# A mixer stage rearranged: gate products inside the Fourier stage, half a weight tile in each attention round, the mixing shares spread by DMA

## The reference

```python
p = u @ w_in[l]                       # u: normed tokens
y_a = fourier_mix(a_in) @ w_br_a[l]   # 8 groups, 2-D DFT, real part
y_b = dilated_mixture(qb, kb, vb, rel_bias[:, :6]) @ w_br_b[l]   # 3 groups, mixed by softmax over their lse
y_c = diff_attention(qc, kc, vc, ...) @ w_br_c[l]                # 4 heads, dense, p0 - lam * p1
gates = sigmoid(u @ w_gate[l] + b_gate[l])                       # 3 gates of width 1024
merged = gates[0] * y_a + gates[1] * y_b + gates[2] * y_c
x = x + merged @ w_out[l]
```

## Time and profile before

| | |
|---|---|
| Runs | 3716.03, 3720.18, 3720.73 us; median 3720.18 us |
| Profiled execution | 3716.92 us, of which the span from first to last instruction is 3715.1 us |
| PE busy | 3500.0 us (94%), mean granted clock 0.969 |
| DVE, ACT, POOL busy | 1602.1 us (43%), 1379.7 us (37%), 1483.0 us (40%) |
| DMA | mean 83 GB/s over the span |
| Chain that ended last | PE 88%, DVE 7%, ACT 2%, issue 2% |

### The profile page before, as it was taken

How to read it: one execution, slowest core, us unless ns; L and a number is a source line. 1 busy time by engine, 2 the same in 40 slices (tenths; PEclk the granted TensorE clock), 3 DMA queues, 4 the chain that set the end, 5 groups by cost and what they waited for, 6 DMA issues and landing times.

```text
span 3715.1 us, 50014 instructions
## 1 busy us (share of the span) xinstructions
PE 3500.0 (94%) x16502; PEld 2868.8 (77%) x16502; DVE 1602.1 (43%) x2305; ACT 1379.7 (37%) x2382; POOL 1483.0 (40%) x1124
## 2 busy tenths in 40 slices
PE   8999997999999999999989999999988987889997
PEld 6888885778888888878857788887777886568886
DVE  3223525644322432244366443224776666243224
ACT  4233323644322432242346443324473233233322
POOL 3444531345444544454313544444220025125443
PEclk9999998999999999999989999999998998989998
DMA  3222321122222322233212323223110012112222
GB/s 111 98 96 96 122 74 44 63 96 96 94 98 96 102 97 96 97 121 102 68 38 68 102 91 101 96 96 102 63 68 10 10 46 85 46 53 100 96 96 91
DMA packets 87302, 309.10 MB, mean 83 GB/s; under 512 B 9823, under 2 KB 11873, under 8 KB 87060
## 3 DMA queue, kind: packets, MB, share of 16 engines
q1 hardware_dynamic: 82512, 297.97, 23.8%
q10 hardware_dynamic: 4676, 9.62, 0.9%
HBM read 305.38 MB, written 2.17 MB: 83 GB/s over the span
## 4 chain that ended last, share of the span: by engine, by line
PE 88%; DVE 7%; ACT 2%; issue 2%; DMA 0%; ACTq 0%; POOL 0%; DVEq 0%; POOLq 0%; SPq 0%
PE ps L438 26%; PE ps L440 25%; PE ps L439 25%; PE ps L843 1%; PE ps L588 1%; PE ps L852 1%; PE ps L611 1%; PE ps L846 1%; PE ps L913 1%; PE ps L601 1%; PE ps L526 0%; PE ps L752 0%; PE ps L898 0%; DVE x L1743 0%; PE ps L731 0%
## 5 line engine op out<-in xcount | busy, mean ns | idle before, releaser
L403 POOL TENSOR_TENSOR w_lo<-raw,w_hi 128x512 fp32r<-128x512 f32 x1120 | 1482.8, 1330 | 2203.2 <-ACT w_hi L943 1726.9
L438 PE MATMUL ps<-u_hi,w_hi 128*128 128x512 f32 (+1 forms) x2990 | 1172.6, 392 | 37.9 <-POOL w_lo L403 10.4
L439 PE MATMUL ps<-u_hi,w_lo 128*128 128x512 f32 (+1 forms) x2990 | 1156.7, 387 | 0.0
L440 PE MATMUL ps<-u_lo,w_hi 128*128 128x512 f32 (+1 forms) x2990 | 1156.4, 387 | 0.0
L438 PEld LDWEIGHTS ps<-u_hi,w_hi 128*128 128x128 f32 x2990 | 566.9, 190 | 164.6 <-issue 28.6
L439 PEld LDWEIGHTS ps<-u_hi,w_lo 128*128 128x128 f32 x2990 | 566.9, 190 | 113.9 <-issue 4.1
L440 PEld LDWEIGHTS ps<-u_lo,w_hi 128*128 128x128 f32 x2990 | 566.4, 189 | 114.1
L945 ACT ACTIVATE w_hi<-raw 128x512 fp32r<-128x512 f32 x560 | 352.5, 629 | 767.7 <-PE ps L440 767.0
L438 PE MATMUL ps<-m_hi,w_hi 128*128 128x512 f32 x1344 | 530.2, 394 | 14.8 <-DVE m_lo L1477 11.9
L943 ACT ACTIVATE w_hi<-raw 128x512 fp32r<-128x512 f32 x560 | 350.8, 626 | 519.4 <-PE ps L440 483.6
L439 PE MATMUL ps<-m_hi,w_lo 128*128 128x512 f32 x1344 | 525.7, 391 | 0.0
(11 more groups left out here) (424 smaller groups left out, 2765.8 us busy)
## 6 DMA issues: line engine op xcount, KB each, us to landing
raw<-jobs SPq DMA_DIRECT2D x560, 512.0 KB, 3.3
tab<-vec_dram ACTq DMA_DIRECT2D x8, 448.0 KB, 5.0
x<-x_in SPq DMA_DIRECT2D x4, 512.0 KB, 6.8
out<-x SPq DMA_DIRECT2D x8, 256.0 KB, 2.0
tab<-dft_in ACTq DMA_DIRECT2D x2, 901.0 KB, 4.8
tab<-chunk_in ACTq DMA_DIRECT2D x1, 1024.0 KB, 4.9
tab<-mem_in ACTq DMA_DIRECT2D x4, 256.0 KB, 3.0
tab<-vec_dram ACTq DMA_DIRECT2D x4, 128.0 KB, 7.1
```

What stands on the lines that cost most here:

```text
L403: pool.tensor_tensor(w_lo[:, s, w], raw[:, s, w], w_hi[:, s, w].bitcast(F32), ALU.subtract).then_inc(lo_done[s], 1)
L438: pe.matmul(ps[bank][:, 0:n], w_hi[:, s, w], hi[:, k, 0:n], start=k == ks[0], stop=False)
L439: pe.matmul(ps[bank][:, 0:n], w_lo[:, s, w], hi[:, k, 0:n], start=False, stop=False)
L440: last = pe.matmul(ps[bank][:, 0:n], w_hi[:, s, w], lo[:, k, 0:n], start=False, stop=k == ks[-1])
```

## The change

- PE runs seven of the first gate's eight jobs inside `fourier`, one in each of the groups 0 to 6, and the eighth after the first scores of `dense`. Their results go to `pt[:, 0:8]`, where the sigmoid is also taken, in the Fourier stage.
- p and q share one bank (`ps[4 + g % 2]`); the sine part's zero column is dropped, and DVE copies the two elements that belonged to it.
- A dense round carries half a job of the Fourier branch (`half_job`): the first half in an even, the second in an odd round. ACT makes one half of the next weights in each round (`split`).
- Probabilities go into `T[:, 7]`, a tile of their own. `logits(u+2)` no longer waits for the transposes of u; `probabilities(u+1)` waits for them.
- The row transposes are spread over the groups 0 to 4 of `fourier`.
- The shares are not spread by PE: ACT's queue stores them to DRAM after round 1 and loads them to 2x64 partitions after round 3. DVE mixes one group in each of the rounds 6, 8 and 10.
- The loads of the first three bias tables are started after the second exponentials and no longer before the first.
- In the tail one gate job stands before heads 0 and 1 and one before heads 2 and 3; the transposes alternate between `ps[7]` and `ps[6]`; ACT writes `m_hi` and DVE `m_lo` straight from PSUM.
- The weight slices lie in DRAM in the new order. Their number is the same.

PE, a new function, `fourier` and `dense`:

```diff
+            def half_job(s, half, hi, lo, ready):
+                if half == 0:
+                    pe.wait_ge(evac[s], c.take(f"evac{s}"))
+                pe.wait_ge(lo_done[s], c.next(f"lo{s}"))
+                for k in range(half * KT // 2, (half + 1) * KT // 2):
...
             def fourier():
...
                     if g < 7:
                         along_channels(g + 1)
+                    if g == 0:
+                        pe.wait_ge(ut_copied, c.now("ut_copied"))
+                        dilated_row(0)
+                    if g < 5:
+                        dilated_row(g + 1)
+                    if g < 7:
+                        job(g % 2, u_hi, u_lo)
...
-                mix_groups(lambda: scores(0))
+                scores(0)
                 pe.wait_ge(vt_done, c.now("vt_done"))
                 scores(1)
+                job(1, u_hi, u_lo)
+                pe.wait_ge(y_done, c.now("y_done"))
                 for u in range(16):
-                    if u < 14:
+                    if 0 < u < 14:
                         scores(u + 2)
...
-                    if u % 2 == 0:
-                        job(0, u_hi, u_lo)
-                    else:
-                        job(1, m_hi, m_lo, ready=(m_ready, c.now("m")) if u == 1 else None)
+                    transposes(u)
+                    if u == 0:
+                        scores(2)
+                    half_job(u // 2 % 2, u % 2, m_hi, m_lo, ready=(m_ready, c.now("m")) if u < 2 else None)
+                    values(u)
                 c.up("m", 8)
-                job(0, u_hi, u_lo)
-                job(1, u_hi, u_lo)
                 for h in range(4):
+                    if h % 2 == 0:
+                        job(h // 2, u_hi, u_lo)
```

ACT, in `dense`:

```diff
                 for u in range(16):
                     act.wait_ge(tr_full, c.next("tr_full"))
                     act.activation(T[:, 4 + u % 2], ps[4][:, :], ACT.Copy).then_inc(tr_copied, c.up("tr_copied"))
+                    split(1 - u // 2 % 2, u % 2)
                     if u % 2:
-                        gate(T[:, 7], T[:, 7], 0, ACT.Sigmoid, bgate(0, u // 2))
-                    pump(1 - u % 2)
...
+                    if u == 1:
+                        act.wait_ge(mixw_done, c.next("mixd"))
+                        act.dma_start(share_dram, rows_m.rearrange("p g n -> p (g n)")).then_inc(shares_stored, c.up("stored", 16))
+                    if u == 3:
+                        act.wait_ge(shares_stored, c.now("stored"))
+                        for h in range(2):
+                            act.dma_start(shares[64 * h:64 * h + 64].rearrange("p g n -> p (g n)"),
+                                          bass.AP(share_dram.tensor, h * 3 * S, [[0, 64], [1, 3 * S]])).then_inc(shares_in, c.up("shares", 16))
```

DVE, in `fourier` and `dense`:

```diff
             def fourier():
                 for g in range(8):
                     if g:
+                        scaled((g - 1) % 2, pt[:, g - 1])
                         fourier_out(g - 1)
...
+                    if g == 6:
+                        dilated_shares(0)
+                        dilated_shares(1)
+                    if g == 7:
+                        dilated_shares(2)
...
                 logits(0)
+                fourier_out(7)
+                fourier_low(6)
+                probabilities(0)
+                fourier_low(7)
+                dve.wait_ge(m_ready, c.now("m"))
                 logits(1)
+                scaled(1, pt[:, 7])
+                logits(2)
+                dilated_shares(3)
```

More of the change, by code:

```diff
@@ L448, in product @@
                 return last
+            def half_job(s, half, hi, lo, ready):
[3 more added lines that the diff above has]
+                for k in range(half * KT // 2, (half + 1) * KT // 2):
+                    if ready:
+                        pe.wait_ge(ready[0], ready[1] + (k + 1))
+                    w = slice(k * P, k * P + P)
+                    pe.matmul(ps[s][:, :], w_hi[:, s, w], hi[:, k], start=k == 0, stop=False)
+                    pe.matmul(ps[s][:, :], w_lo[:, s, w], hi[:, k], start=False, stop=False)
+                    last = pe.matmul(ps[s][:, :], w_hi[:, s, w], lo[:, k], start=False, stop=k == KT - 1)
+                if half == 0:
+                    last.then_inc(job_half[s], 1)
+                else:
+                    last.then_inc(job_done[s], c.up(f"job{s}"))
             def statistic(n=S, squares=acc, bank=7):
@@ L475, in along_channels, with dilated_row @@
                     mm.then_inc(z_full, c.up("z_full"))
+                def dilated_row(i):
+                    if i >= 2:
+                        pe.wait_ge(rows_copied, c.take("rows_copied"))
+                    else:
+                        c.up("rows_copied")
+                    for r in range(4):
+                        mm = pe.transpose(ps[6 if i == 1 else 7][0:2, r * P:r * P + P], (nmax if i < 3 else total)[:, i % 3, r], ident)
+                    mm.then_inc(rows_full, c.up("rows_full"))
                 pe.wait_ge(tab_full, c.next("tab", 128))
@@ L589, in scores, with transposes @@
                     mm.then_inc(sc_full, c.up("sc_full"))
-                mix_groups(lambda: scores(0))
-                pe.wait_ge(vt_done, c.now("vt_done"))
-                scores(1)
-                for u in range(16):
-                    if u < 14:
-                        scores(u + 2)
-                    h = 3 - u // 4
+                def transposes(u):
                     pe.wait_ge(prob_done, c.next("prob"))
@@ L647, in mixers @@
                         pe.wait_ge(evac[s], c.take(f"evac{s}"))
-                        if s == 0:
-                            pe.wait_ge(m_ready, c.now("m") + 5)
-                        product(s, 2 + s, m_hi, m_lo, range(1))
-                        product(s, s, m_hi, m_lo, range(1, 5)).then_inc(job_done[s], c.up(f"job{s}"))
+                        ready = (m_ready, c.now("m")) if s == 0 else None
+                        product(s, 2 + s, m_hi, m_lo, range(1), ready)
+                        product(s, s, m_hi, m_lo, range(1, 5), ready).then_inc(job_done[s], c.up(f"job{s}"))
                 c.up("m", 5)
@@ L1020, in fourier @@
                 act.wait_ge(middle_full, c.next("middle"))
-                act.activation(middle, ps[7][0:8, 0:P], ACT.Copy).then_inc(middle_copied, 1)
+                act.activation(middle, ps[5][0:8, 0:P], ACT.Copy).then_inc(middle_copied, 1)
                 for g in range(8):
@@ L1078, in dense @@
                 exps(0)
+                fourier_out(7)
                 exps(1)
+                load_biases(range(3))
+                c.up("m", 8)
+                last_gate = c.next("evac1")
+                c.up("job1")
                 for u in range(16):
@@ L1441, in _ @@
             dve.sem_inc(y_done, 2)
-            for free in (vt_done, sc_free, wb_free, oT_done, vm_done):
+            for free in (vt_done, sc_free, oT_done, vm_done):
                 dve.sem_inc(free, 1)
@@ L1602, in dilated_shares @@
                 if part == 0:
+                    c.up("rows", 3)
+                    dve.wait_ge(rows_copied, c.now("rows") + 2)
                     dve.wait_ge(mixw_exp, c.next("mixe"))
```

217 lines of the change are left out of this document (105 added, 112 removed).

## The result

The changed kernel takes 3666.39 us (median of 4 runs, 3664.27 to 3670.53), the kernel before beside it 3718.41 us (3716.03 to 3720.73). The ratio is 0.9861, 95% interval 0.9844 to 0.9879. The forecast was 3667 us in a range of 3645 to 3690, with 0.95 on faster. The profiled execution took 3667.71 us, its span is 3665.9 us, 49.2 us less than before. Busy times are now PE 3475.9 us (95%), DVE 1592.1 us, ACT 1348.8 us, POOL 1482.1 us, and the chain that ended last still lies on PE for 88%.

The account below looks back on a forecast made before the run. PE bounds the kernel but waits around the dense rounds. Per mixer 166.6 + 7.0 + 3.5 + 2.5 + 3.0 = 182.6 us against 207.9, so 3716.9 - 50.6 = 3666.3, stated as 3667 us, range 3645 to 3690.

Parts of the forecast that it names:

- PE's own work: Fourier stage, eight gate jobs, sixteen rounds with half a job and tail at full clock: 166.6 us per mixer.
- Fourier stage hides everything: In Fourier groups of 8.8 us on PE, DVE's and ACT's work hides; waits counted as 0.
- To round 2: From the seventh job's end to round 2, PE waits, mainly for DVE's first logits: together 7.0 us per mixer.
- Steady rounds: Dense rounds stay on PE at 5.30 us; mixing in rounds 6, 8 and 10 adds 3.5 us per mixer.
- Tail: PE waits 2.2 us for the heads' scaling, plus 0.3 for the second slot's weights: 2.5 us per mixer.
- Clock: The wait after the first dense scores can bring the clock to 0.50; taken as 3 us lost per mixer.
- The sum: One mixer between its two fixed points takes 182.6 us instead of 207.9: gain 25.3, or 50.6 for two.
- DVE did not become the bound of the rounds: Rival: DVE, held by POOL, bounds the dense rounds, costing 7 us per mixer; time 3681 us, chance 0.19.
- rival 4: Dense rounds stay at 8.02 us because their dependent chain closes inside one round; 3753 us, chance 0.03.
- More is hidden: Rival: no clock loss, mixing at its lower bound, smaller waits; 6 to 9 us less per mixer, 3652, chance 0.11.

Follow-up runs that it names:

- shares_early: Changed kernel with DVE's share work, including the reciprocal, moved one Fourier group earlier; 3664.3 us, ratio 0.9853.
- late_split: Changed kernel with shares earlier, mixing in steps 7, 9, 11, 15, 16, tail square root and head scaling earlier, transposes starting after two scaled heads; 3642.18 us, ratio 0.9799.
- old_tail: Changed kernel with the earlier tail order: both gate jobs first, one transpose bank, ACT through a scratch tile; 3677.17 us, ratio 0.9889.
- again: The changed kernel run and profiled once more, unaltered; 3666.38 us, ratio 0.986.
- whole: Changed kernel with a whole Fourier-branch job in each odd dense round and none in the even ones; 3720.98 us over 10 runs, ratio 1.0009.

## Why the prediction was right, step by step

- **PE's own work.** Forecast 166.6 us per mixer. Measured: 179.79 less the waits (4.06 + 1.04 + 4.38 + 2.19 = 11.67) and less 1.8 for the clock is 166.3. The groups (8.77 for 8.8) and the rounds (5.30 for 5.30) came out as worked out from the earlier trace rows. This is the core of the forecast, and it is no luck.
- **Fourier stage hides everything.** Right: 62.94 of 62.94 us busy at clock 1.00.
- **To round 2.** Forecast 7.0 us, measured 5.10. The wait before the second scores was 4.06 for 4.65, and *shares_early* showed the cause of two thirds of it, DVE's queue with the reciprocal in it. The wait of 1.15 us at round 0's V product did not come: ACT's exponentials of round 1 ended at 663.86 us, the three starts of bias loads lay beside them and not behind them, the copy was done at 664.36, and PE reached its product only at 667.40. The wait before the probabilities of round 1 was 1.04 for 0.8 to 1.2.
- **Steady rounds.** Right: no wait in plain rounds up to round 13. Mixing cost 0.90 + 1.60 + 1.62 = 4.12 for 3.5, near the upper bound of 4.3. The product, the first mixing operation of a step, took 1.06 to 1.07 us each time in place of 0.69, the hold by POOL that the bound allowed for. The wait of 0.26 us in round 14 makes it 4.38 and is not from the mixing: it is also in *late_split* (0.25), which has no mixing there. PE's rounds 14 and 15 hold no scores and are shorter, and the forecast put that at nothing.
- **Tail.** Wait 2.19 for 2.2; the further 0.3 for the second slot's weights did not come. The branch products start 14.9 us after the last V product ended, for 15.4. In *old_tail* three waits of 1.46 to 1.68 us stand between the heads, which the job and the second bank cover in the changed kernel, and the clock behind them falls as it did before.
- **Clock.** Forecast 3, measured 1.8 (13.60 us at 0.87). This and the missing 1.15 are the main terms that were sized too large.
- **The sum.** Forecast 182.6 us and a gain of 25.3 per mixer. Measured 179.8, a gain of 29.0 in the first mixer (with the 3.07 us that the clock lost behind it before) and 27.3 in the second, 56.3 in all, not 50.6. The total still came out at 49.2 less span: the stretches ahead of the two mixers, which the change does not touch, were 4.1 and 5.1 us longer in this execution, and the one behind them 2.2 shorter. In *again* the first was only 0.1 us longer, the second again 5.3. Most of that are clock dips in the dilated stage, and the one profile of before has few of them, so whether the change has a part in the 5 us stays open. The closeness of 3666 to 3667 is in part luck: the mixers gained 5.7 us more than forecast, and stretches that the forecast held fixed took more than that back.
- **Rivals.** DVE did not become the bound of the rounds. The Trainium skill (SBUF — State Buffer, Who interferes with whom) was right on the hold: every mixing product under POOL took 1.06 or 1.07 us. It was too short, and in too few rounds, to decide. The closed chain of rival 4 did not bind with half jobs: a round without any job, in *whole*, took 5.04 us, just under the 5.30 of a round with half a job. That margin is small, and *whole* shows the other side of the forecast, with no gain left, by uneven rounds and not by rounds that stay at 8.02 us. "More is hidden" was partly true (no V wait, less clock), at the price of the mixing.

## What to carry to other kernels

Moving work out of a saturated stage paid here only with what remained spread so evenly that no round fell below the length of the dependent chain (5.04 us of 5.30): the same jobs in every second round gave the whole gain back. After such a move the queues of the engines that were idle decide: ask for each wait which instruction that nobody waits for yet stands ahead of the awaited one, above all where a round has become shorter, and move that. Judge small edits by the length of the touched stage in the trace if totals scatter by more than the edit is worth, and look at the granted clock there before an edit is credited or blamed.

## What the runs showed of the hardware

- **Clock dips in a saturated stretch.** In the dilated stage, which all these kernels share, the granted clock fell to 0.50 (1.2 GHz) for some 3 us with PE busy, behind a group of eight small score products (64 rows by 128 columns, 2.24 us), in some executions and not in others. Windows of the changed kernel and then of *again*, the same kernel:

```profile
540.00:550.00 10.00, 10.00 (x39) 8.25 (x39) 2.89 (x5) 2.08 (x4) 2.31 (x3) 0.83 0.16 52
560.00:570.00 10.00, 10.00 (x41) 8.13 (x42) 3.29 (x5) 2.38 (x4) 3.97 (x4) 0.87 0.17 54
```

```profile
540.00:550.00 10.00, 10.00 (x47) 8.17 (x46) 3.35 (x5) 2.38 (x4) 2.59 (x2) 1.00 0.19 61
560.00:570.00 10.00, 10.00 (x51) 8.43 (x50) 1.98 (x3) 3.04 (x6) 4.35 (x4) 1.00 0.30 102
```

  PE is busy 10.00 of 10.00 us in all four; the changed kernel issued 39 and 41 products, *again* 47 and 51. Its rows in the trace show where:

```profile
539.66 2.24 PE L562 MATMUL ps<-pt 64*128 64x128 f32 x8
...
542.18 0.63 PE L440 MATMUL ps<-u_hi,w_lo 128*128 128x512 f32 x1
...
546.26 0.39 PE L439 MATMUL ps<-u_hi,w_hi 128*128 128x512 f32 x1
```

  and the window between them the level:

```profile
542.20:545.20 3.00, 3.00 (x9) 2.33 (x8) 1.80 (x3) 0.63 (x1) 0.00 (x0) 0.50 0.50 162
```

  Ahead of this dip PE's last wait was at 522.87 us; the one at 560 us has a wait of 0.69 us at 556.58, just before its group of score products.

  The first point of the mixer lay between 580.91 and 587.01 us in the twelve profiles, and those with the late ones show such dips. Why one execution dips and another does not stays open.

- **Holds between POOL and DVE go both ways.** Beside the scalings of *late_split* POOL lost 0.5 us and DVE 2.2 us. In the Fourier stage of the changed kernel POOL's pair took 3.83 us (2.53 at 636.37) beside DVE operations on two partitions, 1.66 us each. With POOL idle a DVE operation of the same shape took 0.67 us (last row):

```profile
642.82 3.83 POOL L404 TENSOR_TENSOR w_lo<-raw,w_hi 128x512 fp32r<-128x512 f32 x2 [3.92 <-ACT w_hi L965]
643.84 1.66 DVE L1652 TENSOR_TENSOR pt<-pt 2x512 f32<-2x512 f32 x1
...
622.65 0.67 DVE L1639 TENSOR_TENSOR pt<-pt 2x512 f32<-2x512 f32 x1
```

- **Starting three loads from ACT's queue delayed no activation here.** The starts (ACTq, 662.35 to 663.64) lie beside the exponentials of round 1, and the copy of round 0's transposes follows right behind these:

```profile
662.35 0.81 ACTq L1163 DMA_DIRECT2D tab<-vec_dram  x2
...
663.77 0.59 ACT L1121 ACTIVATE T<-ps 128x512 f32<-128x512 f32 x1
```

- **A reciprocal on two partitions costs as much as on 128.** The one that held DVE ahead of the first logits took 3.33 us for 2x512; the twelve of 128x512 in the same trace (L1511) took 3.35 us on average.
